# Odd mixer: the output product of seven heads inside the last head's round

## The reference

```python
def _odd_mixer(h_ctx, h_lat, w_in, lower_bounds, layer, out_norm, ctx_out):
    ...                                   # q, i, og and two gates, 8 heads of 128 x 128
    dirs.append(_directional_scan(q, k, i, log_f, n_ctx, reverse=(d == 1)))
    o_lat = _gated_readout(dirs[0][1] + dirs[1][1], og[:, :, n_ctx:], out_norm)   # per head: rms, gate
    ...
# in the block, for this layer
x_lat = x_lat + m_lat[2] * _rms(o_lat @ w_out, norm_post_mix[l])
h_lat = _modulate(_rms(x_lat, norm_pre_ffn[l]), m_lat[3], m_lat[4])
```

## Time and profile before

| what | value |
|---|---|
| median of three runs | 3431.77 us |
| the profiled execution's own time | 3430.91 us |
| its span, first to last instruction | 3429.1 us |
| busy: TensorE / VectorE / ScalarE / GpSimd | 3144.1 / 835.9 / 413.5 / 295.7 us |
| mean granted TensorE clock | 0.956 |
| the last head's round, from its context product to its readout | 1385.1 to 1415.5 us |
| turn, product and seam, up to the first TensorE work of the next stage | 1416.2 to 1463.0 us |

### The profile page before, as it was taken

One profiled execution on the slowest core, in us unless ns is written; L12 is line 12 of the kernel. 1 busy time (PEld: TensorE's weight loads), 2 busy tenths in 40 slices (PEclk: granted clock), 3 DMA queues, 4 the chain that ended last, 5 costly groups with the idle time before them and its releaser, 6 DMA issues.

```text
span 3429.1 us, 41655 instructions
## 1 busy us (share of the span) xinstructions
PE 3144.1 (92%) x18198; PEld 1789.7 (52%) x18198; DVE 835.9 (24%) x1557; ACT 413.5 (12%) x1011; POOL 295.7 (9%) x349
## 2 busy tenths in 40 slices
PE   6988778999988999799988999878999999999997
PEld 2456533444447777477656766444444444444443
DVE  1147921000046667300132000253000000000002
ACT  1024111000022222100021000131000000000001
POOL 1123610000012323200000000000000000000000
PEclk9989889999999999899999999878999999999998
DMA  8660002221021212143412343304898899889883
GB/s 339 250 254 1 1 0 79 93 92 74 37 76 44 62 50 80 46 164 145 159 68 111 130 184 122 118 21 183 342 394 344 344 369 364 347 344 391 346 342 112
DMA packets 204421, 601.94 MB, mean 176 GB/s; under 512 B 5740, under 2 KB 46924, under 8 KB 197712
## 3 DMA queue, kind: packets, MB, share of 16 engines
q1 hardware_dynamic: 199968, 589.45, 45.4%
q0 software_dynamic: 3808, 9.21, 0.8%
q10 hardware_dynamic: 464, 0.60, 0.1%
HBM read 598.19 MB, written 1.05 MB: 175 GB/s over the span
## 4 chain that ended last, share of the span: by engine, by line
PE 79%; DVE 11%; issue 3%; ACT 2%; DMA 2%; POOL 1%; POOLq 0%; PEld 0%; PEldq 0%; ACTq 0%; DVEq 0%
PE ps_ffn_gate L582 10%; PE ps_ffn_up L582 10%; PE ps_ffn_down L618 9%; PE ps_moe_gate L2790 6%; PE ps_moe_down L2835 6%; PE ps_moe_up L2790 6%; PE ps_hg_step L1836 4%; PE ps_project L504 4%; PE ps_lin L1354 3%; PE ps_moe_gate L2795 3%; PE ps_moe_up L2795 3%; PE ps_moe_down L2841 3%; PE ps_lin L296 3%; DVE rec_qd L2059 2%; PE ps_moe_turn L2781 1%
## 5 line engine op out<-in xcount | busy, mean ns | idle before, releaser
L582 PE MATMUL ps_ffn_gate<-hT,ring_buf 128*128 128x256 f32 (+1 forms) x1152 | 343.1, 452 | 4.4 <-issue 2.4
L582 PE MATMUL ps_ffn_up<-hT,ring_buf 128*128 128x256 f32 (+1 forms) x1152 | 336.7, 445 | 1.3
L618 PE MATMUL ps_ffn_down<-ring_buf,ffn_hiddenT 128*128 128x512 f32 x752 | 325.9, 593 | 3.1 <-issue 3.1
L582 PEld LDWEIGHTS ps_ffn_gate<-hT,ring_buf 128*128 128x128 f32 x1152 | 221.8, 193 | 120.3 <-issue 98.9
L582 PEld LDWEIGHTS ps_ffn_up<-hT,ring_buf 128*128 128x128 f32 x1152 | 217.9, 190 | 110.3 <-issue 90.0
L1836 PE MATMUL ps_hg_step<-ring_buf,hT 128*128 128x256 f32 (+2 forms) x1024 | 236.5, 386 | 9.1 <-ACT hg_kT L1925 5.6
L618 PEld LDWEIGHTS ps_ffn_down<-ring_buf,ffn_hiddenT 128*128 128x128 f32 x752 | 141.7, 190 | 182.1 <-issue 182.0
L663 DVE TENSOR_TENSOR ffn_hiddenT<-ffn_silu_buf,ps_ffn_up 128x256 f32<-128x256 f32 (+1 forms) x72 | 36.2, 503 | 750.9 <-PE ps_ffn_up L582 750.9
L1836 PEld LDWEIGHTS ps_hg_step<-ring_buf,hT 128*128 128x128 f32 x1024 | 174.6, 193 | 55.9 <-ACT hg_kT L1925 7.0
L2790 PE MATMUL ps_moe_up<-ring_buf,moe_xg_buf 128*64 128x512 f32 (+1 forms) x1024 | 199.5, 542 | 0.0
L2962 DVE TENSOR_TENSOR moe_hidden_buf<-moe_silu_buf,ps_moe_up 128x768 f32<-128x768 f32 (+1 forms) x32 | 27.3, 854 | 677.3 <-PE ps_moe_up L2795 614.1
(11 more groups left out here) (478 smaller groups left out, 3507.9 us busy)
## 6 DMA issues: line engine op xcount, KB each, us to landing
ring_buf<-in_w_exp_up_dram SPq DMA_DIRECT2D x24, 4096.0 KB, 14.5
ring_buf<-in_w_exp_down_dram SPq DMA_DIRECT2D x24, 4096.0 KB, 14.0
moe_third<-in_w_exp_gate_dram SPq DMA_DIRECT2D x16, 4096.0 KB, 16.3
mod_pieces<-in_mod_w_dram SPq DMA_DIRECT2D x40, 1024.0 KB, 6.4
ring_buf<-in_w_exp_gate_dram SPq DMA_DIRECT2D x8, 4096.0 KB, 17.4
ring_buf<-in_odd_w_in_dram SPq DMA_DIRECT2D x40, 512.0 KB, 5.3
moe_third<-in_w_exp_gate_dram SPq DMA_DIRECT2D x8, 2048.0 KB, 9.1
ring_buf<-in_w_exp_up_dram SPq DMA_DIRECT2D x8, 2048.0 KB, 7.8
```

Of the source, the lines that this page charges most:

```text
L582: mm = nc.tensor.matmul(ps[:, 0:wide], view[:, k, i * P:(i + 1) * P], hT[:, k, first_col:first_col + wide], start=k == 0, stop=k == KD - 1)
L618: mm = nc.tensor.matmul(ps_y[i % 2][:, h, :], hidT[:, b, i * P:(i + 1) * P], view[:, b, h * 512:(h + 1) * 512], start=first, stop=end)
```

## The change

The product of heads 0 to 6 is issued by TensorE inside the round of head 7, and its sums stay in PSUM banks 0 to 3 (two tiles by two halves). `turn_heads` transposes finished heads into bank 4 in the groups (0, 1), (2, 3), (4, 5), (6,), (7,), and `take_heads` on ScalarE copies each group to hT. `project` is told with `begun=bank` that the sums exist: it adds head 7 alone and then runs the seam as before, in the same PSUM. `turn` and its meeting are gone. The loads of `w_out` are issued by the odd mixer's SyncE program, behind its own 16 items.

In the last round all four units use one pair of banks (5 and 6) for their scores, so `scores(U)` waits for `mask(U - 1)` and not for `mask(U - 2)`. There the root and the readout of head 6 stand earlier: on GpSimd between the two halves of the keys, on VectorE behind the first `add_levels`. The readout ends with an increment of `hg_read` and no longer with a wait of VectorE for itself. The second and third load of a ring item increment one semaphore instead of two.

```diff
@@ project
+            if begun is None:
+                ps_y = [pb(cx, f"ps_project{i}", [P, D]) for i in range(2)]
+                turned = [pb(cx, f"ps_turned{i}", [P, KD, P]) for i in range(2)]
+            else:
+                ps_y = [begun[:, 2 * i:2 * i + 2, :].rearrange("p h n -> p (h n)") for i in range(2)]
+                turned = [begun[:, 4 + 2 * i:6 + 2 * i, :].rearrange("p h (k n) -> p (h k) n", n=P) for i in range(2)]
+            k_first = 0 if begun is None else KD - 1
...
-                        for k in range(KD):
+                        for k in range(k_first, KD):
@@ odd_mixer
+            two_banks = lambda lo: bank[:, lo:lo + 2, :].rearrange("p b (l n) -> p (b l) n", n=P)
+            ps_step = [bank[:, i, :] for i in range(3)]
+            LAST = 4 * (HH - 1)
+            scores_of = lambda U: two_banks(3) if U < LAST and U % 2 == 1 else two_banks(5)
+            bank_out = bank[:, 7, :]
+            ps_turned, ps_product = bank[:, 4, :], lambda i, h: bank[:, 2 * i + h, :]
+            GROUPS = [(0, 1), (2, 3), (4, 5), (6,), (7,)]
...
+                for h in range(2):
+                    stream(sp, 2 * HH + h, by_rows(a["odd_w_out"][0])[:, :, h * 512:(h + 1) * 512])
...
                 for h in range(HH):
                     keys(h, 0)
+                    if h == HH - 1:
+                        roots(h - 1)
                     keys(h, 1)
-                    if h >= 1:
+                    if 1 <= h < HH - 1:
                         roots(h - 1)
...
-                    pe.wait_ge(S["rec_masked"].handle, S["rec_masked"].at(max(U - 1, 0)))
+                    pe.wait_ge(S["rec_masked"].handle, S["rec_masked"].at(max(U - 1, 0) if U < LAST else U))
...
                     ahead(("lb", 0), ("f", 0))
+                    if not more:
+                        break
...
+                def turn_heads(g):
+                    pe.wait_ge(Z["hg_read"].handle, Z["hg_read"].at(GROUPS[g][-1] + 1))
+                    if g == 0:
+                        pe.wait_ge(S["rec_masked"].handle, S["rec_masked"].at(LAST))
+                    pe.wait_ge(s_tr["turn_taken"].handle, s_tr["turn_taken"].at(g))
+                    for x, k in enumerate(GROUPS[g]):
+                        for i in range(2):
+                            mm = nc.tensor.transpose(ps_turned[:, (2 * x + i) * P:(2 * x + i + 1) * P],
+                                                     O[:, i, k * P:(k + 1) * P], ident)
+                    mm.then_inc(s_tr["turn_psum"].handle, 1)
+
+                def product(k):
+                    pe.wait_ge(s_tr["turn_taken"].handle, s_tr["turn_taken"].at(k // 2 + 1))
+                    if k == 0:
+                        pe.wait_ge(Z["hg_taken"].handle, Z["hg_taken"].at(len(steps)))
+                    for h in range(2):
+                        if k == 0:
+                            await_item(pe, 2 * HH + h)
+                        for i, t in enumerate(LAT_TILES):
+                            nc.tensor.matmul(ps_product(i, h), hT[:, k, t * P:(t + 1) * P],
+                                             slot_view(2 * HH + h, KD, 512)[:, k, :], start=k == 0, stop=False)
+
+                turn_heads(0)
+                context(HH - 1)
+                product(0)
+                turn_heads(1)
+                product(1)
+                scores(LAST)
+                product(2)
+                scores(LAST + 1)
+                output(LAST)
+                product(3)
+                turn_heads(2)
+                scores(LAST + 2)
+                output(LAST + 1)
+                product(4)
+                scores(LAST + 3)
+                output(LAST + 2)
+                product(5)
+                turn_heads(3)
+                output(LAST + 3)
+                product(6)
+                turn_heads(4)
...
+                for g in range(4):
+                    take_heads(g)
                 square(HH - 1)
+                take_heads(4)
...
-                    link_v(last)
+                    last.then_inc(Z["hg_read"].handle, 1)
...
                     add_levels(u)
+                    if h == HH - 1:
+                        readout(h - 1)
                     mask(u + 1)
@@ rest
-        odd_mixer(O)
-        turn(lambda t, k: O[:, t - 2, k * P:(k + 1) * P], LAT_TILES)
+        odd_mixer(O, bank)
...
+                project(a["odd_w_out"][0], LAT_TILES, Y, GatedSeam(cy, 1, 0, (1, 1), LAT_TILES),
+                        begun=bank)
```

More of the change, by code:

```diff
@@ L468, in passed, with project @@
                 s_norm[k].passed(n)
-    def project(w, tiles, Y, seam, of=lambda k, t: hT[:, k, t * P:(t + 1) * P]):
+    def project(w, tiles, Y, seam, of=lambda k, t: hT[:, k, t * P:(t + 1) * P], begun=None):
         nt = len(tiles)
         with ExitStack() as cx:
-            ps_y = [pb(cx, f"ps_project{i}", [P, D]) for i in range(2)]
-            turned = [pb(cx, f"ps_turned{i}", [P, KD, P]) for i in range(2)]
+            if begun is None:
[5 more added lines that the diff above has]
+            k_first = 0 if begun is None else KD - 1
             S = s_lin
@@ L479, in y_done, with _ @@
                 eng.wait_ge(S["lin_psum"].handle, S["lin_psum"].at(i + 1))
[L480 to L486, removed]
+            gates = [x[:, :, :].rearrange("p k n -> p (k n)") for x in turned] if begun is None else \
+                [begun[:, 4 + 2 * i:6 + 2 * i, :].rearrange("p h n -> p (h n)") for i in range(2)]
+            seam.attach(gates, turned, lambda i: ps_y[i % 2][:, :], lambda i: Y[:, tiles[i], :], y_done)
+            if begun is None:
+                @block.sync
+                def _(sp):
+                    for h in range(2):
+                        stream(sp, h, by_rows(w)[:, :, h * 512:(h + 1) * 512])
             @block.gpsimd
@@ L1637, in program @@
     HH = 8
-    odd_second = [sem(f"odd_second{j}") for j in range(SLOTS)]
-    odd_third = [sem(f"odd_third{j}") for j in range(SLOTS)]
+    odd_others = [sem(f"odd_others{j}") for j in range(SLOTS)]
     c_sig = {n: signal(n, o) for n, o in (
@@ L1730, in _ @@
                         for i, which in enumerate(parts):
-                            landed = (ring_loaded[ring.slot(2 * h + j)], odd_second[(2 * h + j) % SLOTS],
-                                      odd_third[(2 * h + j) % SLOTS])[i]
+                            landed = ring_loaded[ring.slot(2 * h + j)] if i == 0 else odd_others[(2 * h + j) % SLOTS]
                             sp.dma_start(view[:, :, i * P:(i + 1) * P], col(which, h)).then_inc(landed, 16)
+                for h in range(2):
+                    stream(sp, 2 * HH + h, by_rows(a["odd_w_out"][0])[:, :, h * 512:(h + 1) * 512])
             @block.gpsimd
@@ L1829, in step @@
                             n = 2 * h + j
-                            pe.wait_ge(odd_second[n % SLOTS], 16 * (n // SLOTS + 1))
-                            if j == 1:
-                                pe.wait_ge(odd_third[n % SLOTS], 16 * (n // (2 * SLOTS) + 1))
+                            pe.wait_ge(odd_others[n % SLOTS], 16 * sum(1 + m % 2 for m in range(n % SLOTS, n + 1, SLOTS)))
                         width = {"f": 256, "iqo": 384, "i": P}[kind]
@@ L1979, in _, with take_heads @@
                             take(h + 1, kind, t)
+                def take_heads(g):
+                    k, n = GROUPS[g][0], len(GROUPS[g])
+                    act.wait_ge(s_tr["turn_psum"].handle, s_tr["turn_psum"].at(g + 1))
+                    nc.scalar.activation(hT[:, k:k + n, 2 * P:4 * P],
+                                         ps_turned[:, 0:n * 2 * P].rearrange("p (k n) -> p k n", k=n), ACT.Copy)\
+                        .then_inc(s_tr["turn_taken"].handle, 1)
+                for g in range(4):
+                    take_heads(g)
                 square(HH - 1)
+                take_heads(4)
             @block.vector
@@ L2166, in odd_mixer @@
                 Z[k].passed(len(steps))
-            for k in ("hg_forget", "hg_log", "hg_q", "hg_og", "hg_tree"):
+            for k in ("hg_forget", "hg_log", "hg_q", "hg_og", "hg_tree", "hg_read"):
                 Z[k].passed(HH)
+            for k in s_tr:
+                s_tr[k].passed(len(GROUPS))
             Z["bound_exp"].passed(1), Z["bound_ready"].passed(3), loads_ready.passed(2)
@@ L2998, in rest @@
         O = X[:, 0:2, :]
-        odd_mixer(O)
-        turn(lambda t, k: O[:, t - 2, k * P:(k + 1) * P], LAT_TILES)
+        banks = ExitStack()
+        bank = pb(banks, "ps_odd", [P, 8, 512])
+        odd_mixer(O, bank)
         with ExitStack() as cx:
```

16 lines of the change are left out of this document (7 added, 9 removed).

## The result

The changed kernel takes 3408.59 us (median of four runs, 3407.81 to 3411.14) against 3433.59 us before on the same chip (3428.87 to 3435.41). That set lists 3435.41 twice; without the repetition its median is 3431.77, and the ratio goes with that one: 0.9933, 95% interval 0.9922 to 0.9945, which is 23 us less (19 to 27). A second set of five runs gave 3408.93 us against 3430.89 and a ratio of 0.9937 (0.9923 to 0.9950). The forecast was 3412, with 3405 to 3421.

A forecast was written before the change was run, and what follows sets the result against it. TensorE, 79% of the chain of waits, bounds the kernel. Gains of 24.0, 3.7 and 2.0 us against costs of 5.3, 4.6 and 0.3 give 19.5 less than 3430.91: 3411.4, forecast 3412 us, range 3405 to 3420, upper bound 3421.

The forecast's parts named there:

- growth of the round: Last head's round, context product to last output: TensorE's added work makes it 5.3 us longer.
- T: End of tile 2's product behind the last round, forecast at 1425.1; tile 3 is done at T + 1.7.
- next stage, shift: Behind the seam: the next stage begins at 1443.0 instead of 1462.97, 20.0 us less.
- The round as a sum of TensorE: Last round: TensorE works almost without idle time, its products, scores, outputs and transposes summing to 31.4 us.
- handshakes: Last round: some fourteen handshakes without slack, 0.5 us (0 to 1.5) taken off the 20.0 us gain.
- My sign of being wrong, a mask(28) later than 1396.5: Last round: mask(28), forecast at 1396.06, starting later than 1396.5 would show the forecast wrong.
- The narrow place, output(31),: End of the last round: take(30) is done at 1417.1 and TensorE comes to output(31) at 1417.2.
- the product off the path: Behind the last round: the product of 7 heads leaves the path, 24.0 us less.
- The seam's 4.6 us: Seam: tile 3 queues behind tile 2, next stage at T + 17.9 instead of T + 13.3, 4.6 us cost.
- Rival A: Last round: products and the unit's chain take turns, 8.6 us more over three units, gain 11, 3421; chance 0.10.
- B: Seam or first feed-forward block: waits for weights freed 8 us later hand the gain back, 3431; chance 0.05.
- C: Last round: TensorE's clock stays at its lower level, its 31.4 us double, 3448; chance 0.04.

The follow-up runs named there:

- experiments 6 and 7: Changed kernel with eight more product records in the last round: head 1's product issued again, 3417.60 us; head 0's issued twice with values unchanged, 3415.24 us.
- experiment 5: Changed kernel with the root and readout of head 6 back at their old places in the last round: median 3411.76 us.
- Experiment 3: Changed kernel with the products of heads 0 to 6 issued behind output(31), transposes and copies left in the round: 3424.85 us, ratio 0.9983 to the kernel before.
- experiment 8: Changed kernel with both tiles of the seam taken step by step together: 3408.06 us, ratio 0.9937 to the kernel before.
- experiment 10: Changed kernel with both seam tiles together, ring items freed directly behind the product, seven unused matmuls in TensorE's wait: 3400.88 us, 3402.79 us when run again.
- experiment 9: Changed kernel with both seam tiles together and ring items freed directly behind the product: 3404.48 us, ratio 0.9930 to the kernel before.

## Why the prediction was right

Step by step, in the trace of the changed kernel, offsets from the context product:

| step | predicted | measured |
|---|---|---|
| output(31) ends | 32.7 | 32.36 |
| growth of the round | 5.3 | 4.9 |
| gate rows | 37.0 | 36.90 |
| T, tile 2's product ends | 40.0 | 39.95 |
| tile 3's first square | T + 5.9 | T + 6.0 |
| ring items freed, loads issued | T + 9.6 | T + 9.7 |
| tile 3's transposes | T + 14.0 | T + 13.96 |
| next stage | T + 17.9 | T + 17.88 |
| next stage, shift | 20.0 before 0.5 off | 20.06 |

**The round as a sum of TensorE** held, and experiments 6 and 7 show it where the profile alone cannot: 3.43 us of work more is 3.43 us of time more. The order of the waits held too; mask(29) starts at 1401.55, behind the scores by 0.22 us, not behind the readout, and experiment 5 shows that its place is free. What I took off for handshakes, 0.5 us, is not there: TensorE has no gap at all between 1386.04 and 1422. My sign of being wrong, a mask(28) later than 1396.5, needs its base: it starts at 1397.16, but everything in this execution is 0.96 later, and against the context product it moved by 0.14 us.

**The narrow place, output(31),** came out as narrow as computed: VectorE's take(30) ends at 1417.61 and TensorE starts at 1417.71.

**The parts of the gain.** Experiment 3 gives 18.1 us to putting the products into the round and 1.9 to the rest. In my list the product off the path had 24.0, less 5.3 for the round and 0.3: 18.4; the transposes, the copy and the clock had 5.7, less 4.6 for the seam: 1.1. The two together are 19.5 against 20.0 measured, and the difference is the handshakes; the split is off by less than 1 us, and the clock is in both.

**The seam's 4.6 us** is, behind the 5.3 of the round, the largest cost that I named. It is an estimate, since no run has tile 3's seam alone behind the same product; what comes of the order is real: experiment 8 takes 3.1 of it back, experiment 10 4.8 with the clock.

**Rival A** is out: no idle time for TensorE in the round. **B** is out: the up weights were issued at 1435.70 and landed 8.8 us later, and experiment 9 frees them 8 us earlier without any wait that goes. **C** is out here: the clock was 1.00 in the round, though the product goes through four banks between scores in two others. The rule of the Trainium skill that I had set beside it (TensorE: Matmul & The Clock Gate, "A second HAM failure mode: psum-queue depth-cycling") has TensorE idle between its groups when it cycles through banks, and the clock falls by that. Here the cycling is there and the idle time is not (32.36 of 32.36 us busy), so I had set the rule beside a case that lacks its condition: cycling alone did not lower the clock. (The terms of C add up to 1479.6, not 1479.9, and its gate rows should have had the 2.1 us that they take at the lower clock; neither matters.) Where TensorE had real idle time, as in experiment 3's round (0.74) and in the seam (0.50), it did fall.

**Where the forecast was off:** 3412 against 3408.6. The stretch gives 20 us, the medians 22 and 23 in two sets, with 17 to 27 inside their intervals. No step of the table was off by more than 0.4 us. What lies between 20 and the medians I can place in the profiled pair only: there the late stretches were 3.6 us shorter, at values that the kernel before also had in its next execution. That the medians differ for the same reason is not shown. I gave the median of other executions a precision that a single profile does not have; that the forecast lies within 3.4 us of the result is the sum's doing, that the rest was no larger is in part luck.

## What to carry to other kernels

Where one engine's idle time lies between steps that others set, lay out that engine's new order against each wait's time, from rows; as soon as no wait is late any more, the stretch is a plain sum, and every further microsecond of work in it costs its full length. Work that is moved into such a stretch may have been the cover of something else: here the product had hidden a tile's seam, and by my sum 4.6 of 24 us came back as queueing, of which taking both tiles step by step brought 3.1 back. And compare stretches, not spans, where executions of one kernel differ by more than the steps in question.

## What the runs showed that I had not expected

- How long a stage's first records run at the lower clock differs between executions of one kernel: 8.78 and 7.09 us for the same 32 records, with 1.60 and 1.53 us of waiting ahead of them.
- Two drains between two groups of transposes went with more than their gap of 0.23 us: in the profile without them the clock rose within the 16 records, and the stretch and the stage behind were 0.8 and 1.6 us shorter. It is one profile each; that the drains cause all of it was not tested again.
- Matmuls that nobody reads can be worth their place: 0.9 us by seven of them, and 1.7 us in the first sixteen records of the next stage by two more, though the time did not show the latter.
- A GpSimd operation on one column took 1.24 us instead of 0.19 beside a VectorE sum of two SBUF tiles.
